# A two-layer encoder in fp32r pairs: decays, norm pairs, branch start and sums change places, and GpSimd makes the low parts of right operands three to seven

## The reference, cut to what matters

```python
for layer in range(2):
    h = rms_norm(x, norm_g[layer])
    z = h @ w_in[layer]
    qa, ka, va, ga, qr, kr, vr, gr, gm = split_columns(z)
    # attention: 8 query heads, 2 key/value heads of 64
    qa = apply_axial_rope(rms_norm(qa, attn_q_norm[layer]), cos_a, sin_a)
    ka = apply_axial_rope(rms_norm(ka, attn_q_norm[layer]), cos_a, sin_a)
    ya = (silu(ga) * block_attention(qa, ka, va)) @ w_branch_attn[layer]
    # retention: 4 heads of 128, chunks of 128, a forward and a backward scan
    orr = bidirectional_retention(rope(qr), rope(kr) * 128 ** -0.5, vr, lg_f, lg_b)
    yb = (silu(gr) * head_group_norm(orr, ret_gn_w[layer])) @ w_branch_ret[layer]
    x = x + (sigmoid(gate_a) * ya + sigmoid(gate_b) * yb) @ w_out[layer]
return rms_norm(x, final_norm_g)
```

## Time and profile before

| | us |
|---|---|
| median of 3 runs | 1881.97 (1881.45 to 1884.47) |
| profiled execution | 1879.79 |
| its span | 1878.0 |
| TensorE busy | 1765.7 (94%) |
| VectorE busy | 1286.2 (68%) |
| ScalarE busy | 791.3 (42%) |
| GpSimd busy | 670.8 (36%) |
| of the chain that ended last: TensorE, VectorE | 68%, 20% |

### The profile page before, as it was taken

One profiled execution on the slowest core, in us unless ns is written; L12 is line 12 of the kernel. 1 busy time (PEld: TensorE's weight loads), 2 busy tenths in 40 slices (PEclk: granted clock), 3 DMA queues, 4 the chain that ended last, 5 costly groups with the idle time before them and its releaser, 6 DMA issues.

```text
span 1878.0 us, 30204 instructions
## 1 busy us (share of the span) xinstructions
PE 1765.7 (94%) x10592; PEld 1560.9 (83%) x10592; DVE 1286.2 (68%) x2658; ACT 791.3 (42%) x1759; POOL 670.8 (36%) x581
## 2 busy tenths in 40 slices
PE   5799989999999999999998998999999989999986
PEld 5688978899998788887787888889999978888865
DVE  6879678625544386769987877794445553867798
ACT  4368448622222243333344873683222222433333
POOL 0058227624323223223601761485223422232241
PEclk9999999999999999999999999999999999999998
DMA  7000000111011223224130001001011113122322
GB/s 265 23 12 12 27 23 24 36 33 46 22 36 54 102 64 105 79 95 152 45 116 23 23 1 49 12 12 46 24 45 45 45 62 118 58 89 83 131 79 90
DMA packets 136664, 113.07 MB, mean 60 GB/s; under 512 B 16480, under 2 KB 115040, under 8 KB 136544
## 3 DMA queue, kind: packets, MB, share of 16 engines
q1 hardware_dynamic: 134144, 106.20, 17.6%
q10 hardware_dynamic: 2400, 5.31, 0.8%
HBM read 90.52 MB, written 20.97 MB: 59 GB/s over the span
## 4 chain that ended last, share of the span: by engine, by line
PE 68%; DVE 20%; issue 4%; ACT 3%; POOL 2%; DMA 1%; SPq 0%; POOLq 0%; DVEq 0%; ACTq 0%
PE ps L754 16%; PE ps L756 16%; PE ps L755 16%; PE ps L890 5%; PE ps L879 4%; DVE xh L2168 3%; PE ps L903 3%; PE ps L905 3%; DVE hT_lo L2155 2%; PE ps L996 2%; DVE us L1900 2%; PE ps L980 1%; DVE pT_lo L1812 1%; DVE lsum L2146 1%; DVE nmx L1804 1%
## 5 line engine op out<-in xcount | busy, mean ns | idle before, releaser
L754 PE MATMUL ps<-w_hi,hT_hi 128*128 128x256 f32 (+1 forms) x1280 | 391.5, 306 | 13.4 <-DVE hT_lo L1658 4.8
L756 PE MATMUL ps<-w_hi,hT_lo 128*128 128x256 f32 (+1 forms) x1280 | 377.1, 295 | 0.0
L755 PE MATMUL ps<-w_lo,hT_hi 128*128 128x256 f32 (+1 forms) x1280 | 376.8, 294 | 0.0
L754 PEld LDWEIGHTS ps<-w_hi,hT_hi 128*128 128x128 f32 x1280 | 245.1, 191 | 18.5 <-DVE hT_lo L1658 7.0
L755 PEld LDWEIGHTS ps<-w_lo,hT_hi 128*128 128x128 f32 x1280 | 245.4, 192 | 0.3
L756 PEld LDWEIGHTS ps<-w_hi,hT_lo 128*128 128x128 f32 x1280 | 244.8, 191 | 0.0
L610 POOL TENSOR_SCALAR pp<-pp,rrc 128x1024 f32<-128x1024 f32 x128 | 144.0, 1125 | 167.0 <-DVE rrc L1817 160.1
L1812 DVE TENSOR_TENSOR pT_lo<-ps,pT_hi 128x512 fp32r<-128x512 f32 x256 | 164.3, 683 | 26.6 <-ACT pT_hi L1300 25.3
L556 POOL TENSOR_SCALAR w_hi<-raw 128x1024 fp32r<-128x1024 f32 x65 | 69.2, 1064 | 309.6 <-PE ps L756 272.8
L1804 DVE TENSOR_REDUCE nmx<-ps 128x1 f32<-128x1024 f32 x128 | 154.2, 1205 | 2.6 <-PE ps L879 2.6
L890 PE MATMUL ps<-idf,pp 128*128 128x128 f32 x1024 | 140.8, 278 | 15.5 <-DVE pT_lo L1812 9.1
(11 more groups left out here) (215 smaller groups left out, 4131.3 us busy)
## 6 DMA issues: line engine op xcount, KB each, us to landing
raw<-w_in SPq DMA_DIRECT2D x167, 256.0 KB, 3.3
xs<-xh SPq DMA_DIRECT2D x2, 4096.0 KB, 16.5
ys<-y_st SPq DMA_DIRECT2D x32, 256.0 KB, 2.0
hb<-ys SPq DMA_DIRECT2D x16, 512.0 KB, 4.5
xh<-xs SPq DMA_DIRECT2D x8, 1024.0 KB, 7.3
raw<-w_a SPq DMA_DIRECT2D x16, 256.0 KB, 3.1
raw<-w_r SPq DMA_DIRECT2D x16, 256.0 KB, 3.2
w<-w_o SPq DMA_DIRECT2D x4, 1024.0 KB, 6.9
```

The source lines that it names most:

```text
L754: nc.tensor.matmul(outp, ah, bh, start=(start and i == 0), stop=False)
L755: nc.tensor.matmul(outp, ah, bl, start=False, stop=False)
L756: last = nc.tensor.matmul(outp, al, bh, start=False, stop=(stop and i == len(pairs) - 1))
```

## The change

Moves at four places, the last of them with work that changes engines. A product's number p counts from 0, so the title's three to seven are p = 2 to 6.

1. **Decays.** The three groups, cut into five (`decays_start`, `_ratio`, `_series`, `_powers`, `_end`: 2, 5, 6, 9 and 4 operations), leave the first projection loop and stand in the attention loop of layer 0, j = 0, at i = 2, 5, 7, 9 and 13; the two exponentials at i = 4 and 11.
2. **Norm pairs.** `norms` covers tiles 2i and 2i + 1, in four chains instead of three, after `outputs(1)`, `(3)`, `(5)` and `(7)`; rotations stand one tile earlier in part.
3. **Branch start.** `branch(0, 0)` ahead of `update(3, 7)`, the `cross` steps behind `branch(0, 2)` and `(0, 3)`, `turn_out` behind `branch(0, 8)`; the first four products use the banks 2, 0, 1, 3.
4. **Output projection.** GpSimd makes `left_sum(2)` and half 0 of `left_sum(1)`, and `right_lo` of products 2 to 6. The high and low parts of half 0 of product 1's left operand stand earlier, on ScalarE between the last two tanh and on VectorE ahead of `block_end(7)`.

```diff
+A_BANK = (2, 0, 1, 3)
...
+                def left_sum(p, h):
+
+                    x7 = ((L + 1) * K - 1) * N_Q
+                    pool.wait_ge(g_p, x7 + {2: 3, 1: 5}[p])
+                    pool.wait_ge(d_mg, L * N_G + {2: K, 1: 12}[p])
+                    (r, kr, _), (q, kq, sign) = LEFT[p]
+                    nc.gpsimd.tensor_tensor(left_total(p, h), left(r, kr, h), left(q, kq, h),
+                                            ALU.add if sign > 0 else ALU.subtract).then_inc(o_sum, 1)
...
                 right_sum(0, 2)
+                for h in range(2):
+                    left_sum(2, h)
+                left_sum(1, 0)
+
+                def right_lo(p):
+                    pool.wait_ge(o_blo, L * (2 * N_P) + 2 * N_P + 2 * p)
+                    for h in range(2):
+                        pool.wait_ge(o_bhi, L * (2 * N_P) + 2 * p + h + 1)
+                        hi, lo = right_slot(p, h)
+                        nc.gpsimd.tensor_tensor(lo, right_src(p, h), hi.bitcast(F32), ALU.subtract).then_inc(o_blo, 1)
+
                 right_sum(2, 4)
+                right_lo(2)
...
-                update(RH - 1, T - 1)
                 for g in range(N_G):
                     branch(0, g)
-                    if g < 2:
-                        cross(RH - 1, 2 * g)
-                        cross(RH - 1, 2 * g + 1)
-                    if g == 4:
+                    if g == 0:
+                        update(RH - 1, T - 1)
+                    if 2 <= g <= 3:
+                        cross(RH - 1, 2 * g - 4)
+                        cross(RH - 1, 2 * g - 3)
+                    if g == 8:
                         turn_out(RH - 1, 0)
                         turn_out(RH - 1, 1)
...
-                        a, b = ((0, 3), (3, 6), (6, T))[i]
+                        a, b = 2 * i, 2 * i + 2
...
-                        if j == 0 and L == 0:
-                            if t == 2:
-                                decays_start()
-                            if t == 4:
-                                decays_ratio()
-                            if t == 6:
-                                decays_end()
                         outputs(t)
-                        if t == 2:
+                        if t == 1:
                             norms(0)
+                        elif t == 2:
                             rotate(0)
                         elif t == 3:
                             rotate(1)
+                            norms(1)
                         elif t == 4:
                             split(0)
                             rotate(2)
                         elif t == 5:
                             keep_k(0)
                             split(1)
-                            norms(1)
+                            rotate(3)
+                            norms(2)
                         elif t == 6:
-                            rotate(3)
                             keep_k(1)
                             split(2)
+                            rotate(4)
                         elif t == 7:
-                            rotate(4)
                             split(3)
-                            norms(2)
+                            norms(3)
+                            rotate(5)
...
+                        if L == 0 and j == 0:
+                            if i == 2:
+                                decays_start()
+                            elif i == 5:
+                                decays_ratio()
+                            elif i == 7:
+                                decays_series()
+                            elif i == 9:
+                                decays_powers()
+                            elif i == 13:
+                                decays_end()
...
                 left_lo(0)
-                left_sum(2)
                 give(K - 1, 3)
...
                 merge_sum(K - 1, 1)
+                left_lo(1, (0,))
                 block_end(K - 1)
                 left_sum(1)
                 right_lo(1)
-                left_lo(1)
+                left_lo(1, (1,))
                 left_sum(3)
                 add_up(0)
-                right_lo(2)
                 left_lo(3)
                 add_up(1)
-                right_lo(3)
                 left_lo(4)
                 left_sum(5)
                 add_up(2)
                 left_lo(5)
-                right_lo(4)
-                right_lo(5)
                 add_up(3)
                 left_sum(6)
                 left_lo(6)
                 add_up(4)
-                right_lo(6)
```

66 lines of the change are left out of this document (35 added, 31 removed).

## The result

The changed kernel takes 1896.71 us (median of 6 runs, 1896.22 to 1898.88). Beside them the kernel before has 1881.71 us (6 runs, 1877.34 to 1884.47). The ratio is 1.0087, with a 95% interval of 1.0075 to 1.0100: the change costs 15 to 19 us where the prediction had 7 us of gain, and the time lies outside its range. The profiled execution has a span of 1897.0 us against 1878.0.

The account below looks back on a forecast made before the run. TensorE, busy 94%, was taken as the bound, so only its idles, half-speed stretches and tail could be regained. Terms -3.2 + 1 + 2.1 - 17 + 10 = -7.1 gave 1872.7 profiled, 1874.9 us against the median; range 1864 to 1887.

Parts of the forecast that it names:

- The decays in the loop: Attention loop, layer 0, j = 0: pieces mostly fit VectorE's free 0.9 us a step; +1 us, from 0 to +3.
- TensorE has a score block in hand: Attention loop: TensorE has a block of scores in reserve while three decay pieces stick out by 1.3 us in all.
- The first projection: Decays leaving shorten TensorE's idles, less 2.2 us for longer norm chains: -3.2 us, between -5 and -1.
- the six other decay operations: First projection: decay operations beyond the twenty small ones, whose leaving was credited with 0.8 us.
- The norm pairs: Projections after the first: earlier norms cost +0.6 us per j = 1, +0.9 for second-layer j = 0; +2.1, from -2 to +7.
- the wait for the gains: j = 1 projections: VectorE waits about 2.5 us for gqk one tile earlier, with outputs TensorE needs behind it.
- The branch start: Start of branch projections: products moved ahead hide waits of 6.8 us and 1.7 of half speed; -8.5 us per layer.
- The rival that half of it stays: Branch start: cross keeps a 2 to 3 us wait with its half speed in each layer; 1883.4 us, chance 0.18.
- The output projection: VectorE and GpSimd block each other in turns, delaying products 0, 4 and 6; +5 us per layer, -1 to +12.
- VectorE goes first: Output projection: VectorE is never held up and GpSimd's operations stretch; -1 us each, 1862.9 us, chance 0.12.
- GpSimd becomes the bound: Output projection: GpSimd's single queue holds products 2 to 6; +12 us a layer, 1888.9 us, chance 0.15.

Follow-up runs that it names:

- p_decays: The kernel before with only the five decay pieces moved into the attention loop, norms as before: 1887.42 us, ratio 1.0048.
- d_spread: As p_decays, but one decay operation at a time, in two places of a step where VectorE waits for ScalarE: 1878.11 us, ratio 0.9990.
- b_branch_second: p_branch plus the decays two at a time, only ahead of a step's first reciprocal: 1857.79 us, ratio 0.9876 against the kernel before.
- n_late_j1: As p_norms, but for j = 1 the first chain stands behind the outputs of tile 2 again: 1888.49 us, ratio 1.0045.
- n_spare_chain: The kernel before plus a fourth, redundant norm chain of eleven small operations behind rotate(1) at tile 3 of each projection: 1889.19 us, ratio 1.0047.
- p_branch: The kernel before with only the branch start moved: 1861.75 us against 1879.90, ratio 0.9905.
- p_out: The kernel before with only the output projection changed: 1895.87 us, ratio 1.0085.
- o_right_only: The kernel before with only the right low parts of products 2 to 6 on GpSimd, left operands as before: 1895.37 us, ratio 1.0077.
- d_one_input: As p_decays, but the twelve decay operations with two SBUF inputs take one, so decay values are wrong: 1887.82 us, ratio 1.0041.
- p_norms: The kernel before with only the two-tile norm chains and the new places of rotations: 1891.38 us, ratio 1.0050.

## Why the prediction was wrong, point by point

- **The decays in the loop, +1 (0 to +3).** This is the step that failed: 12.0 us, 12.2 in p_decays. Three things were wrong in it. The free time of 0.9 us a step was an average (over the loop itself, 93.9 us with 81.9 busy, it is 0.75); it stands in waits of 0.3 us inside the step, and the pieces were put at its end, straight ahead of the row maximum that ScalarE waits for. This place is what weighs most, since in d_spread the same VectorE time, one operation at a time and elsewhere in the step, costs a quarter. The operations were priced at 0.2 us from a stretch where GpSimd is nearly idle; in the loop GpSimd works 69 of 97 us, and seven of the 26 operations take 0.8 to 1.3. The prediction knew of the blocking and used it in the output projection only. And the idles it makes, 1.7 to 2.5 us, brought two half-speed stretches that were not counted. The term "TensorE has a score block in hand" had no row behind it. d_spread and b_branch_second show the same operations at 3.0 and 1.9 us. What the loop would lose with the pieces at its end and no blocking stays open.
- **The first projection, -3.2 (-5 to -1).** For the decays alone it was too small (-7.2: the idle of 4.68 became 0.75, and the last of 2.11 became 0.61), for both changes too good (+1.3). The 2.2 us of the fourth chain were entered, but not that the early chains bring the other idles back: 3.26, 2.36, 2.73 and 3.28 us stand where p_decays had 0.82, 2.60, 0.75 and 3.06. This was outside the term's range. A slip inside the term changes little: the six other decay operations stand at 0.8 us in it, and at 0.4 and 0.8 where the same paragraphs price them in the loop.
- **The norm pairs, +2.1 for three projections.** Direction right, size off: +2.5 and +2.7 for the two j = 1 where 0.6 each stood. The named mechanism, the wait for the gains, was seen with 2.54 us, as priced, but n_late_j1 took it away and kept the time in layer 0 (2.5 of 2.9) and most of it in layer 1 (1.7 of 2.9); n_spare_chain shows the fourth chain itself, 2.1 and 2.0. The prediction had the 2.2 us in hand and charged them to the first projection only.
- **The branch start, -8.5 in each layer.** Right, measured -9.5 (p_branch). The `cross` wait did close, and the input of `turn_out` came before its turn. The rival that half of it stays fell.
- **The output projection, +5 per layer (-1 to +12).** Mechanism and places right, to the waits: 3.0, 1.0, 4.5 and 2.0 us were read where the steps gave 3.1, 1.8, 5 and 1.3. (Its start of product 1, 1790.7, is 0.6 earlier than its own terms add up to, 1776.9 + 10.9 + 1.7 + 1.8.) The size was low: 6.8 in layer 1 and 9.3 in layer 0 (p_out), still inside the term's range. At the hand-over of layer 0 the lateness of `add_up` became a wait of 5.57 us in p_out, which the steps for layer 1 could not show.
- **The rivals.** "VectorE goes first" fell: GpSimd's pairs show 5.7 to 6.7 us and VectorE's operations stretch too. "GpSimd becomes the bound" was the nearest: product 4 waits for it, and o_right_only puts the loss on its queue; but at 16 us for both layers it is below the 24 of the rival, and by itself would have left the forecast's sign. In the trace the change is 26 us from the forecast sum of -7.1: 11 in the loop, 8.5 in the first projection and the two j = 1, 8 in the output projections with the projection behind the first of them, less 2 at the branch start. With only the loop mended the sum would be +3.9, so either half of the error was enough to turn the sign.

The range reached to +5 on the median. It was too narrow for one reason above all: the loop had 0 to +3, bounds that no row of a single disturbed step supported, and it moved by 12.

## What to carry to other kernels

Work that is moved into a tight loop is priced by the wait in which it stands, not by the loop's average idle time: look for the row with an idle in brackets on that very engine, and put the work directly ahead of the instruction that waits. A small operation of VectorE cost its own 0.2 us where GpSimd did not run; beside a busy GpSimd seven of 26 took 0.8 to 1.3, with one input as with two, so allow for the length of a GpSimd instruction. But where VectorE would have waited anyway, most of that time cost nothing. And when several moves are made, time them apart first: here one part was worth 18 us and the other three hid it.

## What the runs showed of the hardware

VectorE operations on 128x16 with one SBUF input (tensor_scalar) wait for the end of a running GpSimd instruction just as those with two do (0.77 and 1.06 us in place of 0.15 to 0.18), which I had not expected.

The same instructions at the hand-over between layers take two different times, from what only precedes them. In p_decays, whose code is that of before from the first loop on, the small chain of the norm falls beside GpSimd's fills, with eight of its operations at 0.59 to 0.98 us where the kernel before has three at 0.65 to 1.05, and TensorE idles 4.12 us, where before has 1.28 a little later:

```profile
938.94 0.66 DVE L1570 SCALAR_TENSOR_TENSOR rs<-nt,rs 128x4 f32<-128x4 f32 x1
939.63 0.66 DVE L1566 SCALAR_TENSOR_TENSOR nt<-rs 128x4 f32<-128x4 f32 x1
940.32 0.98 DVE L1568 TENSOR_TENSOR nt<-nt,ss 128x4 f32<-128x4 f32 x1
941.33 0.16 DVE L1570 SCALAR_TENSOR_TENSOR rs<-nt,rs 128x4 f32<-128x4 f32 x1
```

```profile
945.63 1.33 PE L777 MATMUL ps<-idf,hb 128*128 128x128 f32 x8 [4.12 <-DVE xh L2175]
```

The stretch is 2.3 us longer there, in p_decays, d_spread and d_one_input alike, and level with before in p_branch and b_branch_second. n_late_j1 and p_norms, with the same code in that stretch, have +0.8 and +6.3, and idles of 1.09 and 4.41 us there. Which of them a change gets was not to be foreseen from its own diff, and what tips it stays open.
